# Half-array products paired within a head: the second token tile in the other row half, value products on both column halves

## The reference

```python
q_l = concatenate([qn_l, qr_l]); k_all = concatenate([k_c, k_l])   # 128 "nope" + 64 "rope" channels
s = einsum('bhqd,bhkd->bhqk', q, k) * scale      # latent queries see all 512 keys, context queries the 256 of the context
p = softmax(s)
o = einsum('bhqk,bhkd->bhqd', p, v)              # v has 128 channels per head
```

## Time and profile before

| | before |
|---|---|
| median of 3 timed runs | 3071.33 us |
| the profiled execution | 3070.39 us |
| its span in the profile | 3068.6 us |
| TensorE busy | 2847.9 us, 93% |
| VectorE busy | 1163.6 us, 38% |
| ScalarE busy | 701.3 us, 23% |
| mean granted TensorE clock | 0.968 |

### The profile page before, as it was taken

The page is one execution under the profiler, slowest core; times in us unless marked ns, Lnnn a source line. Parts: engine busy times, 40 slices in busy tenths (PEclk is TensorE's granted clock), DMA queues, the critical chain, the costliest instruction groups (busy, mean ns, idle before and its releaser), DMA issues. The chain is left out here.

```text
span 3068.6 us, 34189 instructions
## 1 busy us (share of the span) xinstructions
PE 2847.9 (93%) x12390; PEld 1568.3 (51%) x12390; DVE 1163.6 (38%) x2597; ACT 701.3 (23%) x1331; POOL 20.1 (1%) x26
## 2 busy tenths in 40 slices
PE   5999999999999988999989799999979979999997
PEld 3545444444467767887553333333347764444443
DVE  2322387770256664762232333323334322112222
ACT  2333200000155541001151112112123222112121
POOL 0000000000000000000000000000000000000000
PEclk9979999999999988999999899999999989999999
DMA  6122365551222105774003899999912249999993
GB/s 250 71 97 109 145 239 226 225 219 69 110 83 71 68 1 191 304 269 164 14 11 133 330 396 394 391 396 398 364 55 90 95 161 403 398 392 400 397 399 135
DMA packets 101826, 664.39 MB, mean 217 GB/s; under 512 B 10608, under 2 KB 19056, under 8 KB 25072
## 3 DMA queue, kind: packets, MB, share of 16 engines
q1 hardware_dynamic: 98576, 651.74, 54.3%
q0 software_dynamic: 2592, 9.44, 0.8%
q10 hardware_dynamic: 576, 2.10, 0.2%
HBM read 660.09 MB, written 3.15 MB: 216 GB/s over the span
## 5 line engine op out<-in xcount | busy, mean ns | idle before, releaser
L618 PE MATMUL PB<-A,RING 128*128 128x512 f32 (+1 forms) x1408 | 458.4, 489 | 9.8 <-ACT A L498 6.2
L618 PEld LDWEIGHTS PB<-A,RING 128*128 128x128 f32 x1408 | 269.3, 191 | 199.0 <-issue 174.7
L400 DVE SCALAR_TENSOR_TENSOR WORK<-RING,MORE 128x1024 f32<-128x1024 f32 x288 | 335.5, 1220 | 21.1 <-ACT MORE L632 11.8
L451 PE MATMUL PB<-BIG,RING 128*128 (+2 forms) x928 | 310.7, 497 | 5.5 <-PEq L586 3.3
L2293 DVE TENSOR_TENSOR BIG<-BIG,PB 64x512 f32<-64x512 f32 x64 | 44.2, 690 | 711.1 <-ACT BIG L2207 711.1
L2138 PE MATMUL PB<-BIG 128*128 128x512 f32 (+1 forms) x544 | 213.3, 515 | 49.1 <-DVE X L2300 45.6
L451 PEld LDWEIGHTS PB<-BIG,RING 128*128 128x128 f32 x928 | 175.9, 190 | 139.2 <-issue 128.6
L2106 PE MATMUL PB<-RING,BIG 128*64 128x512 f32 x1024 | 227.7, 597 | 0.0
L2300 DVE SCALAR_TENSOR_TENSOR X<-PB,MODS,X 128x256 f32<-128x256 f32 x408 | 176.6, 479 | 42.7 <-PE PB L2138 40.7
L2138 PEld LDWEIGHTS PB<-BIG 128*128 128x128 f32 x544 | 90.9, 190 | 184.6 <-DVE X L2300 107.3
L517 DVE SCALAR_TENSOR_TENSOR X<-PB,MODS,X 128x256 f32<-128x256 f32 x72 | 32.6, 480 | 357.7 <-PE PB L475 357.7
(11 more groups left out here) (350 smaller groups left out, 3387.0 us busy)
## 6 DMA issues: line engine op xcount, KB each, us to landing
RING<-moe_w SPq DMA_DIRECT2D x192, 1024.0 KB, 8.3
RING<-ada_rows SPq DMA_DIRECT2D x72, 1024.0 KB, 6.8
RING<-ffn_w SPq DMA_DIRECT2D x66, 1024.0 KB, 4.8
MORE<-moe_w SPq DMA_DIRECT2D x64, 1024.0 KB, 8.8
A<-moe_w SPq DMA_DIRECT2D x64, 1024.0 KB, 7.4
CST<-moe_w SPq DMA_DIRECT2D x32, 1024.0 KB, 8.9
BIG<-moe_w SPq DMA_DIRECT2D x32, 1024.0 KB, 10.8
RING<-ada_w SPq DMA_DIRECT2D x17, 1024.0 KB, 6.4
```

Of the source, the lines that this page charges most:

```text
L400: dve_.scalar_tensor_tensor(out=JUNK[:, n % 4, :], in0=RING[:, s, b * D:(b + 1) * D], scalar=1.0, in1=WIDE[:, side // 2, w, :], op0=ALU.mu ...
L451: last = pe_.matmul(PB[:, m, 0:tp], tile(s, 2, D)[:, r, m * P:(m + 1) * P], src(2 * i + r), start=first and r == 0, stop=False)
L618: last = pe_.matmul(PB[:, 2 * s + j, 0:t], tile(s, KD, P, j * KD * P)[:, k, :], A[:, k, 0:t], start=k == 0, stop=k == KD - 1)
```

## The change

In `mla`, the rope queries of token tile 1 are written to the other partition half than those of the other tiles: `placed` swaps the two heads of a pair where t is 1, and `query_rows` reads them back. VectorE's one instruction becomes two, one for each head of the pairs. `scores` now runs the 128-partition products of tiles 0 and 1 first, then their two 64-partition products, one in each row half; tiles 2 and 3 follow one after the other as before. `scored` is raised after each tile.

In `even_mixer` the queries of tile 1 are placed in the other half in the same manner (VectorE's 128x512 instruction becomes two of 128x256), so the score products of tiles 0 and 1 lie in different row halves. `weigh` first waits for both `turned` signals of the head and then runs latent (j = 0) and context (j = 1) products alternately, the first on column half 0 and the second on column half 1. ScalarE copies the output in two instructions of 64x256 and not one of 64x512. VectorE waits for all four tiles' scores before the first maximum.

```diff
+    def query_rows(h, t):
+        r = (h + (t == 1)) % 2
+        return slice(r * HD, (r + 1) * HD)
...
 # mla, scores(h)
-                    for t in range(NT):
-                        pe_.matmul(dst, QNT[:, h, own_rows(t)], KNT[:, h, k0:T], start=True, stop=False)
-                        last = pe_.matmul(dst, QRT[r, h // 2, own_rows(t)], KRT[r, k0:T], start=False, stop=True)
+                    def rope(t):
+                        r = query_rows(h, t)
+                        pe_.matmul(spots[t], QRT[r, h // 2, own_rows(t)], KRT[r, first_key(t):T], start=False, stop=True).then_inc(...)
+                    for turns in ((0, 1), (2,), (3,)):
+                        for t in turns:
+                            pe_.matmul(spots[t], QNT[:, h, own_rows(t)], KNT[:, h, first_key(t):T], start=True, stop=False)
+                        for t in turns:
+                            rope(t)
...
 # mla, vector engine
-                        last = dve_.tensor_tensor(query, HROPE[:, 1, :], HROPE[:, 2, :], ALU.add)
+                        for d in range(2):
+                            last = dve_.tensor_tensor(placed(query, ROPE, d, t), in_pair(HROPE[:, 1, :], ROPE, d),
+                                                      in_pair(HROPE[:, 2, :], ROPE, d), ALU.add)
...
 # even_mixer, scores(h) and weigh(h)
+                        r = query_rows(h, t)
+                        pe_.matmul(dst, QT[r, h // 2, own_rows(t)], KG[r, h // 4, first_key(t):T], start=True, stop=True).then_inc(...)
...
                     for j in range(2):
                         pe.wait_ge(sig("turned").sem, sig("turned").at(2 * h + j + 1))
-                        for kt in range(kts):
-                            last = pe_.matmul(PB[r, 6, half(j)], VB[:, 2 * j + kt, g], PTB[h % 2][:, x:x + S], ...)
+                    for kt, j in ((0, 0), (0, 1), (1, 0), (1, 1), (2, 0), (3, 0)):
+                        last = pe_.matmul(PB[j * HD:(j + 1) * HD, 6, half(h % 2)], VB[:, 2 * j + kt, g], PTB[h % 2][:, x:x + S], ...)
...
 # even_mixer, scalar engine
-                    act_.activation(OT[r, h // 2, :], PB[r, 6, :], ACT.Copy).then_inc(sig("carried").sem, 1)
+                    for j in range(2):
+                        last = act_.activation(OT[r, h // 2, half(j)], PB[j * HD:(j + 1) * HD, 6, half(h % 2)], ACT.Copy)
...
 # even_mixer, vector engine
+                    dve.wait_ge(sig("scored").sem, sig("scored").at(NT * (h + 1)))
                     for j in range(2):
-                        dve.wait_ge(sig("scored").sem, sig("scored").at(2 * h + j + 1))
```

More of the change, by code:

```diff
@@ L809, in scores @@
                 def scores(h):
-                    bank, r = 3 * (h % 2), slice((h % 2) * HD, (h % 2 + 1) * HD)
-                    for t in range(NT):
-                        k0 = first_key(t)
-                        dst = PB[:, bank + t, :] if t < 2 else PB[:, bank + 2, (t - 2) * S:(t - 1) * S]
-                        pe_.matmul(dst, QNT[:, h, own_rows(t)], KNT[:, h, k0:T], start=True, stop=False)
-                        last = pe_.matmul(dst, QRT[r, h // 2, own_rows(t)], KRT[r, k0:T], start=False, stop=True)
-                        if t % 2:
-                            last.then_inc(sig("scored").sem, 1)
+                    bank = 3 * (h % 2)
+                    spots = [PB[:, bank + t, :] if t < 2 else PB[:, bank + 2, (t - 2) * S:(t - 1) * S] for t in range(NT)]
+                    def rope(t):
+                        r = query_rows(h, t)
+                        pe_.matmul(spots[t], QRT[r, h // 2, own_rows(t)], KRT[r, first_key(t):T], start=False, stop=True)                             .then_inc(sig("scored").sem, 1)
+                    for turns in ((0, 1), (2,), (3,)):
[3 more added lines that the diff above has]
+                            rope(t)
                 def flips(h):
@@ L1136, in scores @@
                 def scores(h):
-                    bank, r = 3 * (h % 2), slice((h % 2) * HD, (h % 2 + 1) * HD)
+                    bank = 3 * (h % 2)
                     for t in range(NT):
+                        r = query_rows(h, t)
                         dst = PB[:, bank + t, :] if t < 2 else PB[:, bank + 2, (t - 2) * S:(t - 1) * S]
-                        last = pe_.matmul(dst, QT[r, h // 2, own_rows(t)], KG[r, h // 4, first_key(t):T], start=True, stop=True)
-                        if t % 2:
-                            last.then_inc(sig("scored").sem, 1)
+                        pe_.matmul(dst, QT[r, h // 2, own_rows(t)], KG[r, h // 4, first_key(t):T], start=True, stop=True)                             .then_inc(sig("scored").sem, 1)
                 def flips(h):
@@ L1155, in weigh @@
                 def weigh(h):
[L1156 removed]
+                    g = slice(h // 4 * HD, (h // 4 + 1) * HD)
                     if h >= 2:
@@ L1160, in weigh @@
                         pe.wait_ge(sig("turned").sem, sig("turned").at(2 * h + j + 1))
-                        kts = (NT, 2)[j]
-                        for kt in range(kts):
-                            x = 2 * T * j + kt * S
-                            last = pe_.matmul(PB[r, 6, half(j)], VB[:, 2 * j + kt, g], PTB[h % 2][:, x:x + S],
-                                              start=kt == 0, stop=kt == kts - 1)
+                    for kt, j in ((0, 0), (0, 1), (1, 0), (1, 1), (2, 0), (3, 0)):
+                        x = 2 * T * j + kt * S
+                        last = pe_.matmul(PB[j * HD:(j + 1) * HD, 6, half(h % 2)], VB[:, 2 * j + kt, g], PTB[h % 2][:, x:x + S],
+                                          start=kt == 0, stop=kt == (3, 1)[j])
                     last.then_inc(sig("weighted").sem, 1)
@@ L1250, in _ @@
                     act.wait_ge(sig("weighted").sem, sig("weighted").at(h + 1))
-                    act_.activation(OT[r, h // 2, :], PB[r, 6, :], ACT.Copy).then_inc(sig("carried").sem, 1)
+                    for j in range(2):
+                        last = act_.activation(OT[r, h // 2, half(j)], PB[j * HD:(j + 1) * HD, 6, half(h % 2)], ACT.Copy)
+                    last.then_inc(sig("carried").sem, 1)
             @block.vector
@@ L1280, in _ @@
                         dve.wait_ge(sig("row_flipped").sem, sig("row_flipped").at(t - 1))
-                    dve_.tensor_tensor(NTOK[:, b, 0:T], x[:, 0:T], y[:, 0:T], op)
+                    for d in range(2):
+                        dve_.tensor_tensor(placed(NTOK[:, b, 0:T], HD, d, t), in_pair(x[:, 0:T], HD, d), in_pair(y[:, 0:T], HD, d), op)
                     keys = NTOK[:, b, T:6 * P].rearrange("p (g d n) -> p g d n", g=2, d=2)
```

14 lines of the change are left out of this document (10 added, 4 removed).

## The result

The changed kernel takes **3041.79 us** (median of four runs, 3039.81 to 3044.59), the kernel before beside it 3071.43 (3070.69 to 3072.82). The ratio is 0.9901, with a 95% interval of 0.9885 to 0.9916: 29.6 us less. Forecast were 3039 and 3034 to 3051. The profiled execution took 3044.59 (span 3042.6), 25.8 less than the 3070.39 of before. So the profiled execution shows 3.8 us less gain than the medians.

The account below looks back on a forecast made before the run. TensorE was taken to bound the latent mixer, with the even mixer mixed, the ScalarE-VectorE-ScalarE chain just behind. Terms -20.9 latent, -11.5 even, +0.3 VectorE sum to -32.1 us: forecast 3039, range 3034 to 3051.

Parts of the forecast that it names:

- (1): Latent mixer, tiles 0 and 1: scores 1.22 us shorter per head, -7.3 us over six heads at 2.4 GHz.
- B: Matmuls start in strict program order, so a pair costs one more round: 3045 us; chance 0.05.
- D: Latent pairs do not overlap where one half adds onto a whole product: 3053 us; chance 0.04.
- (2, 3): Latent heads 0 and 1: pairing saves 4.6 us cold; clock rises some 4 us in; together -13.6 us.
- Rival A: The clock rises no earlier in either mixer, so pairing saves only at the old clock: 3050 us; chance 0.14.
- (4, 5, 8): Even mixer: scores 1.92 us, value products 1.88, each -0.86; head 0, with the clock up after 4 us, -5.8.
- step (8): Even mixer's head 0: clock up after 4 us, VectorE's scaling sets the flips, head 5.8 us shorter.
- (6): Even mixer: value products wait for the second `turned`, starting 2.68 or 2.62 us after the flips, before 2.32 or 2.24.
- (7): Even mixer: output copy as two 64x256 instructions adds 0.12 us to the chain, bounds 0 and +0.59.
- (9): VectorE's split placement instructions: +0.15 us per place, bounds 0 and +0.69, +0.3 us together.
- rival C: Even mixer: longer TensorE waits let the clock fall to 1.2 GHz and stay; about 3079 us; chance 0.04.

Follow-up runs that it names:

- e3: Changed order of latent products, but tiles 0 and 1 in the same row half so none overlap, even mixer as before the change: 3058.74 us, ratio 0.9958.
- e4: Kernel before with only the even mixer's scores paired; value products, output copy and latent mixer as before: 3064.45 us, ratio 0.9974.
- e6: Changed kernel, but ScalarE in the even mixer computes the next head's exponentials before waiting for and copying this head's output: 3035.07 us, ratio 0.9880.
- e5: Changed kernel, but the even mixer's value products issue three latent ones before waiting for the second `turned` copy: 3039.96 us, ratio 0.9898.

## Why the prediction was right, and where its sizes were off

(1) **Pairs in warm latent heads**: right. From scores(2) to L451 it was 276.19 - 190.90 = 85.29 us, before 295.71 - 203.09 = 92.62: -7.33, predicted -7.3. In e3 the pair is taken away and its 0.85 us with it. This settles rivals B and D. A pair has 1.13 us, two rounds; three rounds would have 1.56 (one of 0.43 more), and no overlap has 1.98, which is e3's. The Trainium skill, "TensorE: Matmul & The Clock Gate", "Part 3: Packing small matmuls", has matmuls start strictly in program order. The traces of this case do not agree: the first instructions of the two products start 7 ns apart, though the second instruction of the first product stands between them and starts 0.8 us later (175.561).

(2, 3) **The first two heads and the clock**: right. From the first scores to scores(2) 190.90 - 171.03 = 19.87 us, before 33.34: -13.47, predicted -13.6. The rise came 4.3 us in ("some 4"), in the even mixer 4.1. Rival A is out. What the prediction left mixed was the reason, and e3 and e4 part it: with the whole products in a row the clock rises without any overlap (e3), and under paired half products it rises without whole ones (e4). Neither the old alternation of the latent mixer, with TensorE never idle, nor the old half products of the even mixer did.

(4, 5, 8) **Even scores and head 0**: right. Scores take 1.92 us (1526.50 to 1528.42 by the next product's start). Head 0 runs from 1505.85 to 1518.35, 12.50, before 18.30: -5.8 as predicted, and before the flips TensorE waited 1.00 us for VectorE's scaling, which step (8) had as what sets them. Value products take 1.84 to the next start, predicted 1.88.

(6) **The wait for the second copy**: right in kind, 0.1 us too small. From flips to value products it is 2.79 us in odd heads and 2.72 in even ones, predicted 2.68 and 2.62. The predicted step let TensorE start as the copies end; it starts 0.15 us later (1523.00 + 1.51 = 1524.51, and 1524.66).

(7) **The output copy and the chain**: the place was right, the size was not. The two 64x256 copies take 0.77 us where one 64x512 took 0.59, and the exponentials start 0.80 behind the first copy (1518.45, 1519.25), where they started 0.49 behind the single one (1561.12, 1561.61). So the copy costs the chain 0.3 and not 0.12: I took the low end of its bounds. From the end of the value products to the flips it is 1521.87 - 1518.35 = 3.52 us, predicted 3.32. With (6) this makes odd heads 8.15 and not 7.88: -0.10, where -0.38 was predicted. Even heads came as said, -1.23 for -1.30.

The **last head** is -0.35 for -0.7, and here a term was missing from the sum: it charged the second copy's wait (6) to heads 1 to 6 and left it out for head 7, which has it too. With its 0.36 the sum would have been -0.38, but that this is what was measured is chance. Against the kernel before, the chain is 0.3 us longer and the wait for the second copy 0.5, the value products with the last copy are 0.7 shorter, and 0.4 came from a place the sum did not look at: the clock falls in both kernels, but costs 1.64 us before (7.70 against e4's 6.06) and 1.24 here (7.05 against e6's 5.81). At the full clock the last head would have gained nothing (9.26 in e4; 3.51 + 5.81 = 9.32).

Heads 1 to 7 gave 4.3 us and not 5.7, and the even mixer 10.14 and not 11.5. In the waits of odd heads the clock stayed at 1.00 (1510.00 to 1571.00), so rival C is out for this kernel.

(9) **VectorE's split placement**: taken at +0.3 us. Nothing shows in the latent mixer, and the wait ahead of the even scores is 3.60 us where it was 3.52: +0.08. Too dear by 0.2.

**What the sum left out.** Predicted -32.1, measured in the profiled execution -25.8. Of the 6.3 between them 1.4 is the even mixer, 0.1 the latent one, 0.5 the stretch between the two, less the 0.3 charged for (9). The rest is outside: 1.3 before the first scores and 3.4 behind the even mixer, 0.2 of it outside the span. The medians differ by 29.6, and the table shows that these outer stretches move by as much between kernels that do not differ there. What sets them, and whether the changed kernel meets the long kind more often (its executions lie near 3040 and near 3044), is open.

## What to carry to other kernels

A pairing on half of the array is worth its rounds only where TensorE is the bound. In the latent mixer 0.85 us a head arrived whole; in every other head of the even mixer nothing of the scores' 0.86 arrived, because ScalarE's next exponentials stood queued behind a copy that waited for TensorE. So before shortening the busy engine, look at what the engine that it waits for does in the meantime: moving the exponentials ahead gave 9.1 us in that mixer's trace (7.0 by the medians), nearly as much as all that the change did there (10.1). And where the clock is low at the start of a stage, the order of products can be worth more than their number: in the latent mixer two thirds of the gain came with e3, which overlaps nothing.

## What the runs showed that I had not expected

- TensorE busy for 27.95 of 28.00 us stayed at 1.2 GHz, and with the same products in another order (e3) it rose some 4 us in. Whether it is the whole products in a row or the fewer switches that count, no run here tells apart.
- A wait of 1.55 us in e5 let the clock fall in heads 3 and 5 and not in head 1, and 1.54 never did in the changed kernel. Each fall cost 1.7 us. A wait of 3.13 us in the last head was followed by a fall in the kernel before and not in e4.
- The kernel's opening and the stage behind the even mixer vary by 3.9 and 5.3 us between kernels that have the same code there (169.5 to 173.4, 1458.99 to 1464.25), more than most terms of the sum.
